# A hybrid encoder trunk with gathered experts: the coefficients of a quarter placed ahead of the routing piece, and a tiny gelu ahead of the first quarter

## The chip, the cores and the metric

The kernel runs on one core of one Trainium2 chip, in fp32. The metric is the device time of one execution in microseconds (us), the median of three runs. In the profile PE is TensorE, ACT is ScalarE, DVE is VectorE, POOL is GpSimd and SP is SyncE; PEld is the weight load of TensorE.

## What is computed

272 tokens (16 learned ones and 256 of the input) of width 1024 pass two layers. Each layer is a mixer and then a PEER expert layer, each with an RMS norm ahead and a residual add behind; one last RMS norm follows. Layer 0's mixer is stick-breaking attention beside a short gated convolution, layer 1's is a Conformer module: a matmul to 2048, a gate, a causal depthwise convolution of 31 taps, a layer norm, silu, and a matmul back. The expert layer, cut to what matters:

```python
q = (y @ w_q).reshape(T, 8, 2, 128)
s = einsum('thpc,pnc->thpn', q, sub_keys)             # two lists of 128 scores a head
val, idx = top_k(s, 16)
cand = val[:, :, 0, :, None] + val[:, :, 1, None, :]  # 16 x 16 pairs
top_val, top_pos = top_k(cand, 16)
expert = take_along_axis(cand_idx, top_pos)           # 16 experts of 16384, a head and token
gate = softmax(top_val)
act = gate * gelu(einsum('thkd,td->thk', u[expert], y))
out = einsum('thk,thkd->td', act, v[expert])
```

## The kernel before, in words

The expert layers are done in steps of 16 tokens: 17 steps for layer 0 (n = 0 to 16) and 16 for layer 1 (n = 17 to 32). In a step the 128 partitions are 8 heads x 16 tokens, and each partition needs 16 experts. GpSimd gathers them one k at a time: one indirect DMA brings for each partition a row of 2048 values, u and v of one expert side by side, 1 MB in all, into one of R = 12 slots of `ring`. A step has four quarters of four k.

**VectorE** runs, for each quarter q of step n, four dots (`dot`, L1197: row u times the token's y, which TensorE has laid out in PSUM, summed into `dots`), each followed by a piece of the mixer's work (`front` for layer 0's attention of later tokens, `side` for the Conformer of the next block of tokens: in its convolution stage two or three taps of L1252). Behind the four dots stands a piece of the routing of later steps: `route_pairs(n + 1)` in quarter 0 (L1157 to L1169), `route_experts(n + 1)` in quarter 1 (L1174 to L1191, which releases the gathers of step n + 1), `finish(n - 2)` in quarter 2 of layer 1 (L1230 to L1235), `route_best(n + 2)` in quarter 3 (L1141 to L1149). Then comes `weights(n, q)`: it waits for the gelu of the quarter, forms `coef` (L1208) and spreads it into `mix` (L1213). In quarter 0 `add_back(n - 1)` follows (L1219), which waits for TensorE's `back`.

**ScalarE** runs `rows(n + 1)` (L456) and `evacuate(n - 1)` (L628: the expert sum out of PSUM into `osb`) at the head of a step, then for each quarter the gelu of four dots (L642), and behind it the mixer's ScalarE work. In the convolution stage that is 20 diagonal matrices a quarter (L569), one for each tap that TensorE does. At the end of a step stand `final_root` (L622, layer 1) and `gates(n + 1)` (L460, an exp). The compiler puts a load of the activation table where the function changes from one table to another.

**TensorE** runs, in a step, `rows(n)` (L833), `values(n - 1, 3)`, `back(n - 1)` (L858), and in each quarter first the mixer's matmuls (`front`, `side`: L668 with streamed weights, L675 column sums, L886 the taps) and then `values(n, q)` (L845), eight matmuls with `mix` against the v halves of four slots. These free the four slots:

```python
mm = pe.matmul(po[32 * j:32 * j + 32, half, :], mix[:, k, :],
               ring[:, slot, D + 512 * half:D + 512 * (half + 1)], start=(q == 0), stop=(q == 3))
if half == 1:
    mm.then_inc(s_vm, 1)
```

**GpSimd** waits for `s_vm` ahead of a gather, and at the first gather of a step also for the expert numbers:

```python
pool.wait_ge(s_idx, n + 1)
for k in range(TOPK):
    i = n * TOPK + k
    if i >= R:
        pool.wait_ge(s_vm, i - R + 1)
```

With 12 slots the gathers 12 to 15 of step n follow `values(n, 0)`, and those 0 to 3 of step n + 1 follow `values(n, 1)`. SyncE streams the mixers' weights in blocks of 512 KB through four buffers. All engines work through their own instructions in the order in which they are written. Layer 1's mixer is computed in two blocks of tokens, in steps 9 to 15 and 17 to 23: the first matmul takes quarters 3 to 6 of such a window, the convolution quarters 7 to 14 (steps 10 quarter 3 to 12 quarter 2, and 18 quarter 3 to 20 quarter 2), mean, variance and silu quarters 15 and 16, the second matmul 17 and 18.

Of the kernel before, what the change touches and what calls it, by code (L numbers as in the profile page):

```python
# [5 lines left out]
P = 128  # L6
# [27 lines left out]
def hybrid_trunk(nc, xT, smalls, wall, uv, out):  # L34
    f32, u32 = mybir.dt.float32, mybir.dt.uint32
    ALU, ACT = mybir.AluOpType, mybir.ActivationFunctionType
# [84 lines left out]
    with ctx:  # L121
        def sb(name, shape, dt=f32):
            return ctx.enter_context(nc.sbuf_tensor(name, shape, dt))
# [37 lines left out]
        epsc = sb("epsc", [P, 1])  # L161
# [18 lines left out]
        grec = sb("grec", [P, 1])  # L180
        dots = sb("dots", [P, TOPK])
        gel = sb("gel", [P, TOPK])
        coef = sb("coef", [P, TOPK])
        mix = sb("mix", [P, TOPK, 2 * GT])
        osb = sb("osb", [P, D])
# [214 lines left out]
        def _(act):  # L400
# [50 lines left out]
            def rows(n):  # L451

                act.wait_ge(s_y, y_ready(n))
                if n:
                    act.wait_ge(s_yr, n)
                act.copy(yg[:, :, :, :], yT[:, :, tokens(n)].unsqueeze(2).to_broadcast([P, C, H, GT])).then_inc(s_yg, 1)  # L456
# [155 lines left out]
            def final(n):  # L612

                act.wait_ge(s_ha, n + 1)
                act.activation(fsq[:, :, :], hT[:, :, tokens(n)], ACT.Square).then_inc(s_fsq, 1)

            def final_root(n):
                m = n - G0
                act.wait_ge(s_fs, m + 1)
                if m:  # L620
                    act.wait_ge(s_fin, m)
                act.activation(frs[:, :], pf, ACT.Sqrt, bias=epsc[:, :], scale=1.0 / D).then_inc(s_frt, 1)  # L622

            def evacuate(n):
                act.wait_ge(s_vm, TOPK * (n + 1))
                if n:
                    act.wait_ge(s_ot, n)
                act.copy(osb[:, :], po.rearrange("p a b -> p (a b)")).then_inc(s_oe, 1)  # L628

            def put(n):  # L630
                m = n - G0
                act.wait_ge(s_fin, m + 1)
                act.dma_start(out[m], fo[:, m % 2, :, :].rearrange("p c t -> p (c t)")).then_inc(s_out[m % 2], 16)

            for n in range(N):
                if n + 1 < N:
                    rows(n + 1)
                if n:
                    evacuate(n - 1)
                for q in range(4):  # L640
                    act.wait_ge(s_dot, TOPK * n + 4 * q + 4)
                    act.activation(gel[:, 4 * q:4 * q + 4], dots[:, 4 * q:4 * q + 4], ACT.Gelu).then_inc(s_gel, 1)  # L642
                    front(4 * n + q)
                    side(n, q)
                    if q == 1 and n > G0:
                        final(n - 1)
                if n > G0:
                    final_root(n - 1)
                if n > G0 + 1:
                    put(n - 2)  # L650
                if n + 1 < N:
                    gates(n + 1)
# [286 lines left out]
        def _(dve):  # L939
# [260 lines left out]
            def weights(n, q):  # L1200

                ks = slice(4 * q, 4 * q + 4)
                if q == 0:
                    dve.wait_ge(s_exp, n + 1)
                    nc.vector.reciprocal(grec[:, :], gsum[:, n % 2:n % 2 + 1])
                    dve.drain()
                dve.wait_ge(s_gel, 4 * n + q + 1)
                nc.vector.scalar_tensor_tensor(out=coef[:, ks], in0=gel[:, ks], scalar=grec[:, :],  # L1208
                                               in1=gexp[:, n % 2, ks], op0=ALU.mult, op1=ALU.mult)
                if n:  # L1210
                    dve.wait_ge(s_vm, TOPK * (n - 1) + 4 * q + 4)
                dve.drain()
                nc.vector.tensor_tensor(mix[:, ks, 0:GT], coef[:, ks].unsqueeze(2).to_broadcast([P, 4, GT]),  # L1213
                                        sel[:, :].unsqueeze(1).to_broadcast([P, 4, GT]), ALU.mult).then_inc(s_m, 1)
# [112 lines left out]
            for n in range(N):  # L1327
                dve.wait_ge(s_yr, n + 1)
                for q in range(4):
                    for i in range(4):  # L1330
                        dot(n, 4 * q + i)
                        front(4 * n + q - 1, i)
                        if q:
                            side(n, q - 1, i)
                        elif n:
                            side(n - 1, 3, i)

                    if q == 0 and n + 1 < N:
                        route_pairs(n + 1)
                    if q == 1 and n + 1 < N:  # L1340
                        route_experts(n + 1)
                    if q == 2 and n > G0 + 1:
                        finish(n - 2)
                    if q == 3 and n + 2 < N:
                        route_best(n + 2)
                    weights(n, q)
                    if q == 0 and n:
                        add_back(n - 1)
                    if q == 2 and n > G0:
                        final_sum(n - 1)  # L1350
# [46 lines left out]
```

## Time and profile before

| what | value |
|---|---|
| median of 3 runs | 1624.63 us (1623.06 to 1624.73) |
| the profiled execution | 1626.37 us, its span 1624.6 us |
| mean granted TensorE clock | 0.774 |
| busy, share of the span | PE 64%, PEld 44%, DVE 69%, ACT 28%, POOL 31% |
| moved by DMA | 649.84 MB, mean 400 GB/s |
| chain that ended last | DMA 40%, PE 26%, DVE 16%, POOL 5%, ACT 5%, issue 5% |

The span is the time from the first to the last instruction of the profiled execution. The shares are means over stages that differ: the first 116 us have no gathers, the steps of layer 0's attention, of the Conformer blocks and the plain steps follow one another. The last line is the chain followed back from the last instruction to what released each piece of work.

### The profile page before, as it was taken

The page shows a single profiled execution, that of the slowest core. Times are in us where ns is not written, and L with a number is a line of the kernel's source. Part 1 is how long each engine was busy: PE and PEld are TensorE (multiplying, and loading weights), DVE is VectorE, ACT ScalarE, POOL GpSimd, SP SyncE. Part 2 cuts the span into 40 slices and gives each one's busy share as a digit, 9 for nine tenths or more (in the row PEclk, how much of TensorE's full clock was granted, in tenths as well). Part 3 has the DMA queues.
Part 4 walks back from the last instruction along what each step waited for, and adds up shares of the span by engine and source line. Part 5 has one row for each costly group of instructions (what it writes and reads, how often), then busy time and mean ns, then how long its engine had stood idle before and what let it go on. Part 6 is the DMA issues. An engine that isn't in the chain of part 4 may idle for free.

```text
span 1624.6 us, 19989 instructions
## 1 busy us (share of the span) xinstructions
PE 1046.7 (64%) x6936; PEld 712.2 (44%) x6936; DVE 1113.1 (69%) x3119; ACT 462.3 (28%) x953; POOL 502.6 (31%) x541
## 2 busy tenths in 40 slices
PE   8996876747644476867573477776576444544454
PEld 8995643525411265756451165655364111211111
DVE  3446768675577765987756765897756777777764
ACT  4101544111011235743121134763222111111110
POOL 0012334322233322333313322332323333333330
PEclk9997868868855799888796579887897566666655
DMA  9969999999999999899999999899999999999994
GB/s 371 355 230 380 417 411 408 419 421 417 418 422 421 421 418 417 352 421 407 420 416 421 421 419 417 353 409 394 415 418 405 422 422 422 421 422 422 421 421 194
DMA packets 106164, 649.84 MB, mean 400 GB/s; under 512 B 11728, under 2 KB 15824, under 8 KB 38480
## 3 DMA queue, kind: packets, MB, share of 16 engines
q0 software_dynamic: 76032, 553.68, 82.4%
q1 hardware_dynamic: 26400, 92.81, 14.7%
q10 hardware_dynamic: 3632, 2.08, 0.4%
q8 instruction: 55, 0.90, 0.2%
q14 instruction: 45, 0.37, 0.1%
HBM read 647.48 MB, written 1.05 MB: 399 GB/s over the span
## 4 chain that ended last, share of the span: by engine, by line
DMA 40%; PE 26%; DVE 16%; POOL 5%; ACT 5%; issue 5%; DVEq 2%; POOLq 0%; ACTq 0%
DMA ring<-in_uv_dram,expert 33%; PE ps L668 13%; DMA wring<-in_wall_dram 8%; DVE ring L1197 7%; PE ps L845 7%; POOL ring L391 5%; ACT side L569 2%; PE ps L858 2%; DVE side L1252 2%; PE ps L675 1%; ACT L460 1%; PE ps L833 1%; DVE picked L1189 1%; DVE mix L1213 1%; PE ps L886 1%
## 5 line engine op out<-in xcount | busy, mean ns | idle before, releaser
L1197 DVE CUSTOM_DVE_ANT_0 ring<-ring,ps 128x1024 f32<-128x1024 f32 x528 | 635.2, 1219 | 321.2 <-DMA ring<-in_uv_dram,expert 250.8
L391 POOL DMA_INDIRECT ring<-in_uv_dram,expert x528 | 500.5, 948 | 1086.6 <-PE ps L845 840.0
L845 PE MATMUL ps<-ring,mix 128*32 128x512 f32 x2112 | 365.6, 827 | 311.4 <-DVE mix L1213 311.2
L845 PEld LDWEIGHTS ps<-ring,mix 128*32 128x32 f32 x2112 | 67.4, 134 | 509.7 <-DVE mix L1213 367.8
L668 PE MATMUL ps<-yT,wring 128*128 128x128 f32 (+1 forms) x1472 | 205.6, 301 | 71.8 <-DMA wring<-in_wall_dram 43.7
L642 ACT ACTIVATE gel<-dots 128x4 f32<-128x4 f32 x132 | 27.1, 205 | 739.2 <-DVE dots L1197 738.8
L668 PEld LDWEIGHTS ps<-yT,wring 128*128 128x128 f32 x1472 | 193.6, 207 | 94.6 <-DMA wring<-in_wall_dram 48.1
L858 PE MATMUL ps<-sel,osb 128*128 128x16 f32 x528 | 84.0, 304 | 78.6 <-ACT osb L628 78.6
L858 PEld LDWEIGHTS ps<-sel,osb 128*128 128x128 f32 x528 | 80.6, 241 | 116.7 <-ACT osb L628 116.7
L569 ACT ACTIVATE side<-ident,params 128x128 f32<-128x128 f32 x310 | 96.5, 389 | 16.0 <-PE ps L886 14.8
L833 PE MATMUL ps<-ident,yg 128*128 128x128 f32 x264 | 49.1, 348 | 71.6 <-DVE dots L1197 71.6
L886 PE MATMUL ps<-side 128*128 128x128 f32 x620 | 83.6, 298 | 2.4 <-ACT side L569 1.8
L886 PEld LDWEIGHTS ps<-side 128*128 128x128 f32 x620 | 79.6, 211 | 10.6 <-issue 10.6
L833 PEld LDWEIGHTS ps<-ident,yg 128*128 128x128 f32 x264 | 41.1, 183 | 73.7 <-issue 73.5
L668 PE MATMUL ps<-yT,ring 128*128 128x128 f32 (+1 forms) x576 | 69.3, 282 | 0.0
L668 PEld LDWEIGHTS ps<-yT,ring 128*128 128x128 f32 x576 | 68.6, 193 | 1.2 <-issue 1.1
L668 PE MATMUL ps<-side,wring 128*128 128x128 f32 (+1 forms) x448 | 59.7, 296 | 10.7 <-ACT side L595 8.1
L642 ACT ACT_TABLE_LOAD x51 | 65.4, 1283 | 1.4
L668 PEld LDWEIGHTS ps<-side,wring 128*128 128x128 f32 x448 | 57.3, 206 | 17.9 <-ACT side L595 10.0
L1252 DVE SCALAR_TENSOR_TENSOR side<-side,params 128x128 f32<-128x128 f32 x180 | 54.2, 349 | 0.0
L628 ACT COPY osb<-ps 128x1024 f32<-128x1024 f32 x33 | 33.3, 1008 | 41.9 <-PE ps L845 41.9
L1197 DVE DVE_READ_ACCUMULATOR2_ANT dots<- 128x1 f32 x528 | 44.0, 83 | 0.0
(207 smaller groups left out, 1043.8 us busy)
## 6 DMA issues: line engine op xcount, KB each, us to landing
wring<-in_wall_dram SPq DMA_DIRECT2D x124, 512.0 KB, 12.2
ring<-in_wall_dram SPq DMA_DIRECT2D x52, 512.0 KB, 13.2
ring<-in_uv_dram,expert POOLq DMA_INDIRECT x528, 16.3
out_dram<-fo ACTq DMA_DIRECT2D x16, 64.0 KB, 6.9
hT<-in_xT_dram ACTq DMA_DIRECT2D x1, 576.0 KB, 15.9
hT<-in_xT_dram SPq DMA_DIRECT2D x2, 256.0 KB, 3.3
params<-in_smalls_dram ACTq DMA_DIRECT2D x1, 380.0 KB, 19.2
params<-in_smalls_dram ACTq DMA_DIRECT2D x1, 50.0 KB, 2.8
```

Of the source, the lines that this page charges most:

```text
L391: pool.indirect_dma_start(out=ring[:, i % R, :], out_offset=None, in_=uv, in_offset=bass.IndirectOffsetOnAxis(ap=expert[:, n % 2, k:k + 1] ...
L460: act.activation(gexp[:, n % 2, :], topv[:, :], ACT.Exp, bias=negm[:, :], accum_out=gsum[:, n % 2:n % 2 + 1]).then_inc(s_exp, 1)
L569: act.activation(diag[:, j % NDIAG, :], ident[:, :], ACT.Identity, scale=convT[:, c, k:k + 1]).then_inc(s_dg, 1)
L628: act.copy(osb[:, :], po.rearrange("p a b -> p (a b)")).then_inc(s_oe, 1)
L642: act.activation(gel[:, 4 * q:4 * q + 4], dots[:, 4 * q:4 * q + 4], ACT.Gelu).then_inc(s_gel, 1)
L668: last = pe.matmul(ps[:, m % 2, 0:w], weights_at(i)[:, c, :], rhs(c), start=(c == 0), stop=(c == C - 1))
L833: last = pe.transpose(yrep[:, c * P:(c + 1) * P], yg[:, c, :, :].rearrange("p h t -> p (h t)"), ident[:, :])
L845: mm = pe.matmul(po[32 * j:32 * j + 32, half, :], mix[:, k, :], ring[:, slot, D + 512 * half:D + 512 * (half + 1)], start=(q == 0), stop=( ...
L858: last = pe.matmul(pt[:, c, :], osb[:, c * P:(c + 1) * P], sel4[:, :], start=True, stop=True)
L886: mm = pe.matmul(ps[:, m % 2, 0:P], diag[:, j % NDIAG, :], gz[:, c, o0 + k:o0 + k + P], start=(k == 0), stop=(k == CK - 1))
L1197: nc.vector.tensor_tensor_reduce(out=row, in0=row, in1=yrep, scale=1.0, scalar=0.0, op0=ALU.mult, op1=ALU.add, accum_out=dots[:, k:k + 1]) ...
L1252: ins = nc.vector.scalar_tensor_tensor(out=cv[:, c, :], in0=src, scalar=tap, in1=cv[:, c, :], op0=ALU.mult, op1=ALU.add)
```

## The change

`weights(n, q)` moves ahead of the routing piece of its quarter, and a gelu of one column (of a constant, into a tile nobody reads) stands on ScalarE at the head of each step, ahead of the first quarter's wait for its dots. Nothing else differs; there are 33 more instructions, all on ScalarE, and as many table loads as before.

```diff
+        warm = sb("warm", [P, 1])
...
                 if n:
                     evacuate(n - 1)
+
+                act.activation(warm[:, :], epsc[:, :], ACT.Gelu)
                 for q in range(4):
                     act.wait_ge(s_dot, TOPK * n + 4 * q + 4)
...
                         elif n:
                             side(n - 1, 3, i)
 
+                    weights(n, q)
                     if q == 0 and n + 1 < N:
                         route_pairs(n + 1)
                     if q == 1 and n + 1 < N:
...
                         finish(n - 2)
                     if q == 3 and n + 2 < N:
                         route_best(n + 2)
-                    weights(n, q)
                     if q == 0 and n:
                         add_back(n - 1)
```

VectorE at the end of step 10 (the third quarter's last taps, `route_best(12)`, the coefficients of quarter 3, the first dot of step 11), before:

```order
L1252 SCALAR_TENSOR_TENSOR side<-side,params 128x128 [waits s_chain] x2
L1141 MAX val<-ps 128x8 [waits s_sc]
L1141 MAX val<-ps 128x8
L1144 MAX_INDEX idx<-val,ps 128x8
L1145 MATCH_REPLACE rest<-val,ps 128x128
L1144 MAX_INDEX idx<-val,ps 128x8
L1145 MATCH_REPLACE rest<-val,ps 128x128
L1149 MAX val<-rest 128x8 x2
L1208 SCALAR_TENSOR_TENSOR coef<-gel,grec,gexp 128x4 [waits s_gel]
L1213 TENSOR_TENSOR mix<-coef,sel 128x4x16 [waits s_vm]
L1197 ISA ring,dots<-ring,ps 128x1024 [waits s_g8,s_yr]
```

The same place on VectorE with the change (lines below the added ones are counted three further):

```order
L1255 SCALAR_TENSOR_TENSOR side<-side,params 128x128 [waits s_chain] x2
L1211 SCALAR_TENSOR_TENSOR coef<-gel,grec,gexp 128x4 [waits s_gel]
L1216 TENSOR_TENSOR mix<-coef,sel 128x4x16 [waits s_vm]
L1144 MAX val<-ps 128x8 [waits s_sc]
L1144 MAX val<-ps 128x8
L1147 MAX_INDEX idx<-val,ps 128x8
L1148 MATCH_REPLACE rest<-val,ps 128x128
L1147 MAX_INDEX idx<-val,ps 128x8
L1148 MATCH_REPLACE rest<-val,ps 128x128
L1152 MAX val<-rest 128x8 x2
L1200 ISA ring,dots<-ring,ps 128x1024 [waits s_g8,s_yr]
```

The pair of `coef` and `mix` has moved up past the whole of `route_best`; the wait for the gelu (s_gel) now stands ahead of the route's rows. In quarter 0 it moves in the same way past the eleven rows of `route_pairs`, in quarter 1 past those of `route_experts`.

ScalarE at the head of step 11, before:

```order
L460 ACTIVATE gexp,gsum<-topv,negm 128x16 [waits s_top]
L456 COPY yg<-yT 128x1024 [waits s_yr,s_y]
L628 COPY osb<-ps 128x1024 [waits s_ot,s_vm]
L642 ACT_TABLE_LOAD
L642 ACTIVATE gel<-dots 128x4 [waits s_dot]
L569 ACTIVATE side<-ident,params 128x128 [waits s_dgu] x20
```

And with the change:

```order
L461 ACTIVATE gexp,gsum<-topv,negm 128x16 [waits s_top]
L457 COPY yg<-yT 128x1024 [waits s_yr,s_y]
L629 COPY osb<-ps 128x1024 [waits s_ot,s_vm]
L642 ACT_TABLE_LOAD
L642 ACTIVATE warm<-epsc 128x1
L645 ACTIVATE gel<-dots 128x4 [waits s_dot]
L570 ACTIVATE side<-ident,params 128x128 [waits s_dgu] x20
```

The table load stands at the same place in both; the tiny gelu comes between it and the gelu of the quarter.

## Rows read from the trace of the kernel before

**Rows 1.** Windows: stretch, its length, busy us by engine, PEclk, DMA share, GB/s

```profile
148.00:151.00 3.00, 0.27 (x4) 0.00 (x0) 2.91 (x7) 0.00 (x0) 1.90 (x3) 0.50 0.45 147
...
1034.00:1039.00 5.00, 5.00 (x45) 3.45 (x44) 4.54 (x14) 4.14 (x15) 0.99 (x1) 1.00 0.13 49
...
1121.00:1123.00 2.00, 0.00 (x0) 0.00 (x0) 2.00 (x4) 1.47 (x4) 1.70 (x2) 1.00 0.36 152
...
1260.00:1600.00 340.00, 161.23 (x780) 59.81 (x772) 245.26 (x655) 59.41 (x105) 124.03 (x132) 0.62 1.01 421
636.00:735.00 99.00, 73.24 (x515) 57.54 (x513) 87.97 (x264) 62.45 (x171) 34.58 (x36) 0.85 0.95 392
...
1014.00:1140.00 126.00, 91.28 (x643) 72.47 (x644) 108.47 (x315) 73.52 (x190) 40.99 (x43) 0.82 0.95 385
```

**Rows 2.** Waits over the whole span: us in total, times, longest us

```profile
POOL ring L391 <- PE ps L845: 840.0, 127, 16.8
...
DVE ring L1197 <- DMA ring<-in_uv_dram,expert: 250.8, 186, 3.6
...
DVE coef L1208 <- ACT gel L642: 14.2, 20, 3.2
```

**Rows 3.** Timeline of ACT, plain step 26: start us, us, instruction, idle before

```profile
1332.72 1.28 ACT L642 ACT_TABLE_LOAD   x1
...
1336.34 0.21 ACT L642 ACTIVATE gel<-dots 128x4 f32<-128x4 f32 x1 [2.33 <-DVE dots L1197]
```

**Rows 4.** Timeline of ACT and DVE, first quarter of work, step 0

```profile
142.86 0.20 ACT L642 ACTIVATE gel<-dots 128x4 f32<-128x4 f32 x1
...
144.26 0.23 DVE L1213 TENSOR_TENSOR mix<-coef,sel 128x64 f32<-128x64 f32 x1
```

**Rows 5.** Timeline of ACT and DVE, end of step 10, first convolution block

```profile
629.26 5.96 ACT L569 ACTIVATE side<-ident,params 128x128 f32<-128x128 f32 x20
...
631.27 0.50 DVE L1141 MAX8 val<-ps 128x8 f32<-128x128 f32 x2 [1.21 <-PE ps L824]
...
633.09 0.49 DVE L1149 MAX8 val<-rest 128x8 f32<-128x128 f32 x2
...
636.53 0.20 ACT L642 ACTIVATE gel<-dots 128x4 f32<-128x4 f32 x1
...
636.77 0.22 DVE L1208 SCALAR_TENSOR_TENSOR coef<-gel,grec,gexp 128x4 f32<-128x4 f32 x1 [3.19 <-ACT gel L642]
...
637.21 1.22 DVE L1197 CUSTOM_DVE_ANT_0 ring<-ring,ps 128x1024 f32<-128x1024 f32 x1
```

**Rows 6.** Timeline of ACT and DVE, quarter 0 of step 11

```profile
644.39 0.09 DVE L1157 MATCH_VALUE_LOAD idx<-val,rest 128x8 f32 x1
...
647.07 0.43 DVE L1169 MAX8 topv<-cand 128x8 f32<-128x256 f32 x1
...
647.44 0.21 ACT L642 ACTIVATE gel<-dots 128x4 f32<-128x4 f32 x1
...
649.82 0.29 DVE L1219 TENSOR_TENSOR hT<-hT,ps 128x128 f32<-128x128 f32 x1 [1.61 <-PE ps L858]
650.02 1.22 DVE L1197 CUSTOM_DVE_ANT_0 ring<-ring,ps 128x1024 f32<-128x1024 f32 x1
```

**Rows 7.** Timeline of DVE and ACT, quarter 1 of step 21, second block

```profile
1125.09 0.42 DVE L1174 FIND_INDEX8 topp<-topv,cand 128x8 uint32<-128x256 f32 x1
...
1126.03 0.21 ACT L642 ACTIVATE gel<-dots 128x4 f32<-128x4 f32 x1
```

**Rows 8.** Timeline of POOL: first gather of four after a wait, at four places

```profile
148.49 0.94 POOL L391 DMA_INDIRECT ring<-in_uv_dram,expert  x1 [8.70 <-PE ps L845]
...
755.56 0.94 POOL L391 DMA_INDIRECT ring<-in_uv_dram,expert  x1 [11.39 <-PE ps L845]
...
1120.95 1.35 POOL L391 DMA_INDIRECT ring<-in_uv_dram,expert  x1 [11.05 <-PE ps L845]
...
1137.42 0.94 POOL L391 DMA_INDIRECT ring<-in_uv_dram,expert  x1 [11.39 <-PE ps L845]
```

## The prediction

> **What bounds the kernel now.** I looked first at the windows, for the share that the DMA engines are busy stage by stage [rows 1]. In the plain steps at the end, 1260 to 1600 us, it is 1.01 at 421 GB/s, while DVE works 245 of 340 us. There a step lasts as long as its 16 MB of gathers take, and VectorE's order cannot matter as long as the next gathers are issued before the queue is empty. In the two convolution stages (636 to 735 and 1014 to 1140 us) the share is 0.95, and DVE is busy 88 of 99 and 108.5 of 126 us. The shortfall lies in short holes: the DMA is at 0.45 in 148 to 151 us, at 0.13 in 1034 to 1039 us, at 0.36 in 1121 to 1123 us. Only in such a hole can a gather that is issued earlier end the kernel earlier, and one that is issued later costs time at once.
>
> Then I read the waits [rows 2]. GpSimd waits 840 us for the matmuls on `ring` that free slots; VectorE waits 250.8 us for gathers, and only 14.2 us for gelus. The last number is the one to look at, since it is small because the routing piece stands between the dots and the coefficients.
>
> **The change, part by part.** *The tiny gelu.* What is the load of its table worth on the path? In a plain step the load starts at 1332.72 us and takes 1.28 us, and the gelu of the quarter starts at 1336.34 us, after 2.33 us in which ACT waited for the dots [rows 3]. The load is already done before the dots are; in the order of before it stands ahead of the wait as well. The Trainium skill says otherwise (page "ScalarE: Activation LUTs", section "Step-by-step: what each stage is for"): the compiler places a table load right before the activation that needs it, and a switch costs about 2.7 us with its drain. By that rule the load would follow the wait, and bringing it early would pay in every step; the trace does not agree with it. By the row, the gain is nothing. The cost is 33 gelus of at most 0.20 us, the length of the gelu of four columns [rows 5]. ACT waits for the dots in the plain steps, which hides it; where ACT is behind, at the heads of some six steps, half of a gelu's length is a fair price, since operations on ACT overlap, and half of these again is covered. **+0.3 us.**
>
> *Coefficients earlier, plain steps.* `mix` comes 0.5 to 4 us earlier, slots come free as much earlier, and the DMA is full anyway. The routing piece ends 0.4 to 0.7 us later, being pushed by the gelu's latency and the two operations: from the start of a gelu to VectorE's next operation behind `mix` it is 636.53 to 637.21, 0.68 us [rows 5]. VectorE has 95 of 340 us free there. **0.**
>
> *The first step.* The gelu starts at 142.86 us and `mix` at 144.26 us [rows 4]. With 0.68 less 0.14 us behind the gelu `mix` would start at 143.4 us, 0.8 us earlier. The gathers that this frees start at 148.49 us, after 8.70 us of waiting [rows 8], and the DMA is nearly idle then. **-0.8 us.** VectorE itself comes out later, since `route_pairs` now stands behind the gelu that ACT delays; but its own next gathers have three in the queue ahead of them.
>
> *The convolution stages.* ACT is the late engine here: it builds 20 diagonals a quarter, 5.96 us each time [rows 5], and a gelu stands behind them. VectorE used these waits for routing. At the end of step 10 `route_best` ran from 631.27 to 633.58 us and VectorE then waited 3.19 us more for the gelu of 636.53 us [rows 5]. With the change it waits all the time and runs `route_best`'s 2.3 us afterwards, so the dots of step 11 begin 2.2 us later than 637.21 us. That alone is hidden, because the next gelu is set by ACT at 647.44 us, 3 us after `route_pairs` began, so later still behind the dots [rows 6]. But the same happens again there: `route_pairs` ran from 644.39 to about 647.5 us, before that gelu. Now it follows: 647.44 + 0.1 (tiny gelu) + 0.68 + 3.1 + 0.2 (from the add of L1219 to the dot) = 651.5 us instead of 650.02 us, **+1.5 us**. `back` was ready at 649.82 us, so it doesn't hide this [rows 6]; the wait of 1.61 us for it goes away, and `route_pairs` takes its place.
>
> Who waits? The dots of the next quarters, and behind them the gelu, and behind the gelu in ACT's order the next 20 diagonals, `gates` and `evacuate`, and behind these TensorE's `back`, taps and `values`. Earlier coefficients don't help here, since `values` stands behind the taps on TensorE. In step 12 (or 20) the shift is about 1.7 us, and the head of step 13 (or 20 already, where `route_pairs` was hidden altogether) adds 1.4 us more: 3.1 to 3.2 us. In quarter 1 of step 21 the gelu of 1126.03 us is again ACT's, and `route_experts`, which began at 1125.09 us [rows 7], moves behind it: 1126.03 + 0.68 - 1125.09, less the 0.6 that `coef` and `mix` took anyway, is **+1.0 us** more. The second matmul's results wait for VectorE behind that.
>
> What it costs is read where gathers are short. In the second block the first gather after a wait is at 1120.95 us, when the DMA is already in its hole [rows 1, 8]; 3.2 us later is 3.2 us lost, and the next, at 1137.42 us, is 4.2 us later, some of which the weight blocks fill. I take **+3.4 us**, with bounds of 1.5 (if half is absorbed, as in the first block) and 4.5. In the first block the like place is at 755.56 us [rows 8], 2.9 us later; the DMA is full until then, so I take half of it, **+1.5 us**, with bounds of 0 and 3. The hole of 1034 to 1039 us stays as it is: its gelus are ACT's and their `values` stand behind the taps.
>
> Sum: +0.3 - 0.8 + 3.4 + 1.5 = **+4.4 us**. On the profiled execution of 1626.37 us that gives 1630.8 us; the median of the runs is 1.7 us lower, so it is **1629.0 us**. The order at the very end (the last quarter has no routing piece) is the same, and the tail with it.
>
> **The rivals.** *Hidden: no change.* The DMA holds the time from end to end, and VectorE's shifts are taken up by the row of slots that are filled ahead. For it: VectorE is idle in every stage, and the DMA is 40% of the chain that ended last. Against it: the holes, where the queue is empty and the shift passes through. It decides if more than two thirds of the shift of 3 to 4 us is absorbed in each block. Time: from -0.8 + 0.3 to 1.5 us more, 1624 to 1626 us.
>
> *Faster: the holes close.* Slots come free up to 4 us earlier. If the holes were `mix`'s, the change would fill them: 0.55 of 3 us at 148, 0.64 of 2 us at 1121, 0.87 of 5 us at 1034 and as much again in the first block, 1.7 + 1.3 + 2 x 4.4 = 11.7 us at most [rows 1]. Most of these follow `values` that stood behind taps, not behind `mix`; I would give it 4 to 5 us, 1620 us. It decides if TensorE turns out to reach `values` before `mix` is there.
>
> *Faster: the table.* If the load of 1.28 us [rows 3] did sit behind the dots, the eight steps in which VectorE, ACT and TensorE set the pace (0, 1, 11 to 13, 19 to 21) would gain it each: 10 us, 1614 us. The rows speak against it. The rule of the Trainium skill named above would lead here.
>
> *Much slower.* No absorption anywhere: both blocks at 4.2 us and the delay of attention's first steps, some 2.3 us, as well: 1635 us.
>
> **How the numbers follow.** About 0.2% (3.2 us) is what a measurement of this kernel can tell from no change. Forecast (+3.3 to +8 us) 0.56, hidden 0.30, holes close 0.09 (of it 0.02 within 0.2%), table 0.01, much slower 0.04. So slower 0.60, same 0.32, faster 0.08. The range takes in the forecast with its bounds (-0.8 + 0.3 + 1.5 + 0 = +1.0 to +7.0, and 1 more for what I may have missed in the attention steps) and the hidden case: 1623.5 to 1633.0 us.
>
> **What would show it.** VectorE's wait for gelus must grow from 14.2 us to 40 or more. The wait of `add_back` for `back` must go in steps 11, 13, 19 to 21. The gathers of 1120.95 and 1137.42 us must come about 3 and 4 us later against those of 1034 to 1039 us, the hole in front of them must widen, and the plain steps must keep 1.01 and 421 GB/s. Table loads: as many, as early as now. I am wrong if the two blocks last as long as before, or if the first gather behind 1100 us comes earlier.

## The result, and the profile after

| what | before | after |
|---|---|---|
| median (runs) | 1624.27 us (6 runs, 1623.06 to 1625.49) | 1635.07 us (6 runs, 1630.73 to 1636.16) |
| ratio to before, 95% interval | | 1.0064 (1.0051 to 1.0077) |
| the profiled execution, its span | 1626.37, 1624.6 us | 1634.59, 1632.9 us |
| granted TensorE clock | 0.774 | 0.781 |
| VectorE's wait for gelus | 14.2 us, 20 times | 63.1 us, 104 times |
| table loads for the gelus | 51 | 51 |

The change makes the kernel slower by 0.64%: 10.8 us by the medians, 8.3 us by the spans of the two profiled executions. The forecast was +4.4 us and its range ended at 1633.0 us: the sign and the place were right, the size was not.

Windows of the kernel after, the stretches of [rows 1] (stretch, its length, busy us by engine, PEclk, DMA share, GB/s):

```profile
148.00:151.00 3.00, 0.00 (x0) 0.00 (x0) 2.86 (x9) 0.00 (x0) 2.39 (x3) 0.50 0.55 147
636.00:735.00 99.00, 72.24 (x509) 56.79 (x508) 87.06 (x267) 63.25 (x174) 34.82 (x36) 0.84 0.96 393
...
1126.00:1128.00 2.00, 1.46 (x16) 0.24 (x8) 1.97 (x3) 1.10 (x2) 0.28 (x1) 1.00 0.03 12
1128.00:1130.00 2.00, 0.00 (x0) 0.00 (x0) 2.00 (x3) 2.00 (x6) 1.69 (x2) 1.00 0.38 53
...
1014.00:1140.00 126.00, 84.36 (x599) 66.69 (x599) 104.09 (x312) 75.52 (x197) 39.44 (x41) 0.84 0.93 376
...
1260.00:1600.00 340.00, 153.26 (x784) 57.09 (x787) 247.81 (x670) 62.45 (x116) 126.44 (x135) 0.64 1.01 421
```

The plain steps keep 1.01 and 421 GB/s, as forecast. The stretch of the first convolution is the same within 0.01, that of the second fell from 0.95 to 0.93 of the DMA's time: 2% of 126 us is 2.5 us, and more lies behind 1140 us. The hole in front of the gather (21,3) is wider: it was 0.36 in 1121 to 1123 us, and is now 0.03 in 1126 to 1128 and 0.38 in 1128 to 1130 us.

Waits after (engine line, what it waited for, us in total, times, longest), which answer to [rows 2]:

```profile
ACT gel L645 <- DVE dots L1200: 799.3, 114, 12.5
POOL ring L392 <- PE ps L848: 743.0, 110, 16.0
...
DVE ring L1200 <- DMA ring<-in_uv_dram,expert: 242.2, 190, 3.8
POOL ring L392 <- DVE expert L1194: 220.8, 19, 113.2
...
DVE coef L1211 <- ACT gel L645: 63.1, 104, 6.7
```

The wait for gelus has grown by 49 us, in 84 more places. GpSimd's wait for `values` fell by 97 us, and it now waits 19 times for the expert numbers instead of once (113.0 and now 113.2 us of it before the first gather): slots do come free earlier, and at the head of 18 steps the first gather then stands for `route_experts`, which the change has put behind the coefficients.

### The profile page after: what moved, and what is told of

It reads as the page before. It is cut to its first block, busy times and chain, and to the rows that moved or that the text cites. A ratio compares the mean times of both kernels' runs of the same rounds, so it can differ in the third digit from the quotient of the medians.

```text
span 1632.9 us, 20023 instructions
## 1 busy us (share of the span) xinstructions
PE 1052.5 (64%) x6936; PEld 719.9 (44%) x6936; DVE 1115.4 (68%) x3119; ACT 466.2 (29%) x986; POOL 500.1 (31%) x541
## 4 chain that ended last, share of the span: by engine, by line
DMA 42%; PE 25%; DVE 15%; ACT 7%; POOL 5%; issue 4%; DVEq 1%; POOLq 0%; ACTq 0%
DMA ring<-in_uv_dram,expert 37%; PE ps L671 13%; DVE ring L1200 8%; DMA wring<-in_wall_dram 6%; POOL ring L392 5%; PE ps L848 5%; ACT side L570 2%; PE ps L861 2%; DVE side L1255 1%; PE ps L678 1%; PE ps L836 1%; PE ps L889 1%; ACT osb L629 1%; ACT L461 1%; DVE picked L1192 1%
## 5 line engine op out<-in xcount | busy, mean ns | idle before, releaser
L671 PE MATMUL ps<-yT,wring 128*128 128x128 f32 (+1 forms) x1472 | 213.6, 309 | 67.5 <-DMA wring<-in_wall_dram 35.7
L671 PEld LDWEIGHTS ps<-yT,wring 128*128 128x128 f32 x1472 | 201.9, 215 | 88.8 <-DMA wring<-in_wall_dram 42.3
L1211 DVE SCALAR_TENSOR_TENSOR coef<-gel,grec,gexp 128x4 f32<-128x4 f32 x132 | 29.3, 222 | 65.1 <-ACT gel L645 63.1
L678 PE MATMUL ps<-side,ones 128*128 128x128 f32 (+1 forms) x144 | 29.3, 385 | 25.3 <-ACT side L600 13.8
```

Of the source, the lines that this page charges most:

```text
L671: last = pe.matmul(ps[:, m % 2, 0:w], weights_at(i)[:, c, :], rhs(c), start=(c == 0), stop=(c == C - 1))
L678: last = pe.matmul(ps[:, m % 2, 0:w], ones[:, :], src[:, c, 0:w], start=(c == 0), stop=(c == C - 1))
```

## Where the time came from

The first gather of a group of four is a good clock of progress, since it can't be issued before slots are free. Its time in the two traces, from the timelines of GpSimd (step and quarter of the gathered experts):

| gather | before | after | later by |
|---|---|---|---|
| 11, 3 | 659.32 | 659.29 | 0.0 |
| 14, 0 | 755.56 | 758.43 | 2.9 |
| 16, 0 | 854.56 | 855.28 | 0.7 |
| 20, 1 | 1051.31 | 1053.39 | 2.1 |
| 20, 3 | 1078.76 | 1082.68 | 3.9 |
| 21, 3 | 1120.95 | 1127.72 | 6.8 |
| 22, 0 | 1137.42 | 1146.73 | 9.3 |
| 32, 3 (the last four) | 1585.33 | 1593.59 | 8.3 |

Up to the end of the first block most is as forecast, and only the gain of the first step doesn't last: the 0.6 us won in the first step (148.49 to 147.90 us) is gone at 659 us, the gather of 755.56 us comes 2.9 us later, and the full DMA behind it takes most of that back. The second block does not: 7.2 us are lost between the gathers (20,1) and (22,0) alone, where 3.4 us were forecast for the whole block.

The head of step 20, quarter 0, before (the order's own wait for `back`, in front of the first dot of quarter 1):

```profile
1067.54 0.21 ACT L642 ACTIVATE gel<-dots 128x4 f32<-128x4 f32 x1
...
1067.67 0.43 DVE L1169 MAX8 topv<-cand 128x8 f32<-128x256 f32 x1
...
1069.91 0.29 DVE L1219 TENSOR_TENSOR hT<-hT,ps 128x128 f32<-128x128 f32 x1 [1.15 <-PE ps L858]
1070.12 1.21 DVE L1197 CUSTOM_DVE_ANT_0 ring<-ring,ps 128x1024 f32<-128x1024 f32 x1
```

The same place after:

```profile
1070.34 1.28 ACT L642 ACT_TABLE_LOAD   x1
1071.63 0.20 ACT L642 ACTIVATE warm<-epsc 128x1 f32<-128x1 f32 x1
1071.74 0.19 ACT L645 ACTIVATE gel<-dots 128x4 f32<-128x4 f32 x1
...
1071.96 0.22 DVE L1211 SCALAR_TENSOR_TENSOR coef<-gel,grec,gexp 128x4 f32<-128x4 f32 x1 [3.04 <-ACT gel L645]
...
1075.27 0.43 DVE L1172 MAX8 topv<-cand 128x8 f32<-128x256 f32 x1
1075.61 0.27 DVE L1222 TENSOR_TENSOR hT<-hT,ps 128x128 f32<-128x128 f32 x1
1075.80 1.22 DVE L1200 CUSTOM_DVE_ANT_0 ring<-ring,ps 128x1024 f32<-128x1024 f32 x1
```

From the gelu to the next dot it was 2.58 us and is 4.06 us. Before, all of `route_pairs` but its last MAX8 had run when the gelu started; now the 3.04 us of waiting that held it are empty, and its 3.1 us follow. That is the forecast mechanism, and at step 11 it has the forecast size (the dot of [rows 6] moves from 650.02 to 651.57 us). But the gelu itself is 4.20 us later here, which the forecast did not have. The same reading at the places where ScalarE brings the gelu late:

| place | gelu later by | next dot later by |
|---|---|---|
| step 10, q1 | 0.2 | 1.6 |
| step 11, q0 | 0.1 | 1.6 |
| step 12, q0 | 1.8 | 1.8 |
| step 13, q0 | 1.4 | 2.9 |
| step 13, q1 | 1.6 | 2.9 |
| step 18, q1 | 1.3 | 2.8 |
| step 19, q0 | 2.6 | 4.1 |
| step 20, q0 | 4.2 | 5.7 |
| step 21, q0 | 6.6 | 8.0 |
| step 21, q1 | 6.4 | 7.7 |

Of these places four in the first block and five in the second add 1.2 to 1.5 us to the shift that they find; step 12 adds none. In the first block that of step 10 is gone by the next gelu (615.46 us in both traces). In the second, 1.3 us were there on entry, and the shifts of step 18 to the head of step 21 stay and come one on top of the other. In quarter 3 of steps 10 and 18 VectorE comes 2.2 us later as well, but the next gelu does not. In quarter 1 of steps 11, 19 and 20 VectorE was as late already, and at most 0.3 us are added. The second block's heads are longer on ScalarE, since `final_root` (a table load of 1.28 us and 0.28 us) stands there too, and `route_pairs` lay almost wholly within the wait at each of them. And step 19 is entered with 2.6 us: in quarter 1 of step 18, in the stage of the first matmul, `route_experts` filled such a wait as well (the gelu of 977.27 us came 2.5 us behind its dots), and the forecast has no term for it. The next matmul of the mixer on TensorE starts 2.4 us later there (984.69 and 987.09 us); by which wait the shift reached it was not followed.

Then quarter 1 of step 21, where the second matmul's chunks go through two PSUM banks. Timeline of TensorE before:

```profile
1124.77 5.47 PE L668 MATMUL ps<-side,wring 128*128 128x128 f32 x32 [4.07 <-ACT side L595]
1131.01 3.81 PE L668 MATMUL ps<-side,wring 128*128 128x128 f32 x32 [0.77 <-DVEq L1309]
1134.74 1.92 PE L845 MATMUL ps<-ring,mix 128*32 128x512 f32 x16
```

and after:

```profile
1131.21 3.84 PE L671 MATMUL ps<-side,wring 128*128 128x128 f32 x32 [3.76 <-ACT side L596]
1138.69 5.44 PE L671 MATMUL ps<-side,wring 128*128 128x128 f32 x32 [3.63 <-DVEq L1312]
1144.05 1.92 PE L848 MATMUL ps<-ring,mix 128*32 128x512 f32 x16
```

A group of 32 is two chunks. The second two wait until VectorE has read the banks of the first two, which it does between the dots of quarter 2, behind `route_experts`. From start to start of the two groups it was 6.24 us and is 7.48 us, 1.24 us more, and that is what VectorE comes later behind the gelu (gelu to next dot 3.29 us before, 4.53 us after). The wait in brackets has grown by more, 0.77 to 3.63 us, since the first group was quicker; and the second now takes 5.44 instead of 3.81 us. The gathers of step 22 wait for the `values` behind it. Timeline of GpSimd after (the like of the last line of [rows 8]):

```profile
1127.72 1.03 POOL L392 DMA_INDIRECT ring<-in_uv_dram,expert  x1 [11.37 <-PE ps L848]
...
1146.73 0.94 POOL L392 DMA_INDIRECT ring<-in_uv_dram,expert  x1 [14.26 <-PE ps L848]
```

## The experiments

Most are the changed kernel with the place of `weights(n, q)` chosen quarter by quarter, the tiny gelu kept:

```diff
-                    weights(n, q)
+                    early = CONDITION
+                    if early:
+                        weights(n, q)
                     if q == 0 and n + 1 < N:
                         route_pairs(n + 1)
...
                         route_best(n + 2)
+                    if not early:
+                        weights(n, q)
```

The chips differ: in the first four runs and the last two the kernel before took 1625.2 and 1624.75 us, in the others 1632.4 to 1633.2 us. Every ratio is to the kernel before on the same chip. Beside the ratio I read two stretches from each trace: **A**, from the gather (20,1) to (21,3), which holds the head of step 20 and that of step 21 up to its first coefficients, and **B**, from (21,3) to (22,0), which holds quarter 1 of step 21. Most of the 8 us between the chips lie ahead of both, but A is not free of it: with the old order there it is 70.5 us on the faster chips (mean of 5 traces) and 71.8 us on the slower (4).

### Which part, and where

```diff
-                act.activation(warm[:, :], epsc[:, :], ACT.Gelu)
```

with `early = True`:

> The change without the tiny gelu: only the coefficients placed ahead of the routing piece. Theory A (VectorE now waits, in the two convolution blocks, for gelus that ScalarE has late, and does its routing afterwards): the whole loss stays, 8 to 11 us over before, 1633 to 1635 us, the first gather behind 1120 us of before again 6 to 7 us late. Theory B (ScalarE's extra operation at the head of a step carries the loss, since ScalarE is the late engine in the blocks): most of it goes, 1624 to 1627 us.

`early = False`, the tiny gelu kept:

> The tiny gelu alone, the order of before. Theory A: 33 operations of 0.2 us, mostly where ScalarE waits anyway, and the table load as early as before: 1624 to 1625 us, no change. Theory B: slower by 5 us or more.

`early = n not in (10, 11, 12, 13, 18, 19, 20, 21)`:

> The change's order everywhere except in steps 10 to 13 and 18 to 21, which have the order of before; with the tiny gelu. Theory A: the loss is made in these eight steps only, so 1623 to 1626 us. Rival C (the delay of VectorE adds up over all steps, the attention steps above all): 3 us or more slower than before, 1628 us or more.

`early = n in (10, 11, 12, 13, 18, 19, 20, 21)`:

> The reverse: the change's order in steps 10 to 13 and 18 to 21 only. Theory A: the whole loss, 1632 to 1635 us. Rival C: less than half of it, under 1629 us.

| kernel | median, us | ratio (95%) | A, us | B, us |
|---|---|---|---|---|
| before | 1625.2 | | 69.64 | 16.47 |
| after | 1635.07 | 1.0064 (1.0051 to 1.0077) | 74.33 | 19.01 |
| e1, order only | 1631.15 | 1.0048 (1.0031 to 1.0064) | 72.48 | 17.71 |
| e2, tiny gelu only | 1624.98 | 1.0002 (0.9994 to 1.0011) | 69.20 | 16.46 |
| e3, outside the blocks | 1624.1 | 0.9994 (0.9985 to 1.0003) | 71.12 | 16.29 |
| e4, inside the blocks | 1634.45 | 1.0060 (1.0046 to 1.0073) | 74.14 | 19.09 |

The order inside eight steps makes the loss by itself. In the other 25 steps it makes no difference that can be measured, and neither does the tiny gelu alone. Whether the gelu adds something to the order stays open: e1 is 0.16% under the change, the intervals overlap, and in e1's trace the second group of B's matmuls ran at the higher clock, which is part of the distance (below).

### Which block, which quarter

`early = n in (18, 19, 20, 21)`:

> The change's order in steps 18 to 21 only (second convolution block), tiny gelu as in the change. The prediction gave the second block 3.4 us and the first 1.5. From the trace of the change, where the gathers are 1.5 us late behind the first block and 8 to 9 behind the second: about 6 to 7 us over before here, 1631 us. If the two blocks only add up in the way that the prediction had them: 1628.5 us.

`early = n in (10, 11, 12, 13)`:

> The change's order in steps 10 to 13 only (first block). 1.5 to 2.5 us over before, 1626 to 1627.5 us. If the blocks weigh the same: 4 to 5 us.

The steps of both blocks, quarter 0 alone:

> The change's order in steps 10 to 13 and 18 to 21, in quarter 0 alone: the coefficients ahead of route_pairs. The prediction puts the shifts there: three times 1.5 us in a block (steps 11, 12, 13), one of them absorbed by the layer norm's wait, so 3 us at the hole and over half of the loss: 1628 to 1631 us. If the late release of the second matmul's banks behind route_experts in quarter 1 of steps 13 and 21 is the larger part: under 1627 us.

and quarter 1 alone:

> The same in quarter 1 alone: the coefficients ahead of route_experts. By the prediction 1 us in a block: 1625.5 to 1627 us. If TensorE's wait for VectorE in quarter 1 of step 21 (3.63 us with the change, 0.77 before) is the quarter's own doing: 1628 us or more.

| kernel | median, us | ratio (95%) | A, us | B, us |
|---|---|---|---|---|
| e5, second block | 1638.91 | 1.0034 (1.0020 to 1.0049) | 72.54 | 17.71 |
| e6, first block | 1633.38 | 1.0004 (0.9992 to 1.0015) | 71.45 | 16.22 |
| e7, quarters 0 | 1634.58 | 1.0014 (1.0003 to 1.0025) | 73.56 | 16.05 |
| e8, quarters 1 | 1636.21 | 1.0025 (1.0015 to 1.0036) | 71.65 | 19.34 |

The second block costs 0.34%, 5.5 us; the first 0.04%, which is 0.6 us and can't be told from nothing. Both are under what had been expected of them, and e7's 0.14% (2.3 us) is under the half of the loss that was expected of quarter 0. Quarter 1 costs at least as much as quarter 0, and the stretches separate them cleanly: e7 lengthens A and leaves B, e8 lengthens B by 2.9 us and has A where the old order has it (e6). A and B are one trace each.

### Quarter 1 of step 21

`early = (n, q) not in ((13, 1), (21, 1))`:

> The whole change, but in quarter 1 of steps 13 and 21 (the second matmul of each Conformer block) the coefficients stay behind route_experts, as before. Theory P (route_experts behind the late gelu makes TensorE's second pair of chunks wait 3.63 us for VectorE's bank release instead of 0.77, and run at the low clock, 5.44 instead of 3.81 us): the wait returns to about 1 us, the second pair to 3.8 us, values(21,1) come 3 to 5 us earlier than with the change against values(21,0), and the time is about 1629 to 1631 us on a chip where the change takes 1635. Rival S (the delay is a plain sum of shifts of about 1 us spread over all quarters of the blocks): these two quarters give back at most 1.5 us, 1633.5 us or more.

`early = (n, q) == (21, 1)`:

> The order of before everywhere but in quarter 1 of step 21, which has the order of the change. Theory P: this one place costs 1 us of VectorE's shift, 1 to 3 us of TensorE's wait and 1.6 us if the pair falls to the low clock: 1626.5 to 1629 us where before takes 1624.6. Rival S: at most 1 us, 1625.6 us. Rival C (the loss at this place needs the shift collected in steps 18 to 20): no change, 1624.6 us, and the second pair stays at 3.8 us.

The change, and `route_experts` moved away from in front of the bank release:

```diff
-                    if q == 1 and n + 1 < N:
+                    if q == 1 and n + 1 < N and n not in (13, 21):
                         route_experts(n + 1)
...
                         elif n:
                             side(n - 1, 3, i)
+                        if n in (13, 21) and q == 2 and i == 1:
+                            route_experts(n + 1)
```

> The change, but route_experts for steps 14 and 22 is moved from behind the dots of quarter 1 to behind the second dot of quarter 2 and its piece of the mixer, so that both PSUM banks are released ahead of it. Theory P (the bank release behind route_experts is the cause in quarter 1 of step 21): TensorE's second pair of chunks waits under 1 us instead of 3.63, gathers (21,3) to (22,0) are 16.5 us or less instead of 19.0, and the time is 2 to 3 us under f0. Rival E (route_experts itself then comes too late for the gathers of step 22): GpSimd's first gather of step 22 waits for expert instead of values, and the time is that of f0 or more. Rival S (spread): no change against f0.

The change itself once more, beside it on the same chip:

> The change itself, so that the next three stand beside it on one chip. If this is the chip of the first runs: ratio 1.006 to the kernel before. On the slower chip, where parts of the change cost 0.04% to 0.34%: 1.003 to 1.004, and the stretch from gather (21,3) to gather (22,0) is 19 us as in the change's first profile (16.5 before).

| kernel | median, us | ratio (95%) | A, us | B, us |
|---|---|---|---|---|
| e9, the change without the two quarters | 1635.79 | 1.0025 (1.0011 to 1.0039) | 72.56 | 16.46 |
| e10, one quarter alone | 1636.5 | 1.0019 (1.0005 to 1.0032) | 71.89 | 18.91 |
| f0, the change again | 1640.46 | 1.0045 (1.0029 to 1.0060) | 72.72 | 17.71 |
| f1, the change, experts later | 1637.26 | 1.0023 (1.0006 to 1.0040) | 74.05 | 15.30 |

In e9 the wait of TensorE's second group is 0.76 us and the group takes 3.81 us, as theory P had it. Its ratio is 0.20% under that of f0, on another chip, and the intervals overlap. One quarter of one step, moved by itself (e10), costs 0.19% (3.1 us); theory P gave 1.9 to 4.4 us for it. B of f0 is 17.71 us and not the 19 that had been expected, since its second group ran at the higher clock. Timeline of TensorE in e10:

```profile
1132.92 3.84 PE L671 MATMUL ps<-side,wring 128*128 128x128 f32 x32 [3.65 <-ACT side L596]
1140.40 5.44 PE L671 MATMUL ps<-side,wring 128*128 128x128 f32 x32 [3.64 <-DVEq L1312]
```

and in f1:

```profile
1134.52 9.04 PE L671 MATMUL ps<-side,wring 128*128 128x128 f32 x64 [3.91 <-ACT side L596]
1143.49 1.92 PE L848 MATMUL ps<-ring,mix 128*32 128x512 f32 x16
```

e10 shows the change's lines with nothing else moved, so the shift collected in steps 18 to 20 is not needed for it. In f1 the wait is gone: the four chunks run as one group of 64 in 9.04 us, where before they took 10.05 us from the start of the first group to the end of the second, and after 12.92 us. B falls to 15.30 us, under that of the kernel before, and rival E (the expert numbers come too late) doesn't hold: GpSimd waits there 10.39 us for `values`. f1 is 3.2 us under f0 by the medians, as theory P had it; the intervals of the two ratios overlap a little, the stretches don't.

### The other places

`early` everywhere but in ten quarters, 1 of step 10, 0 of 11 to 13, 1 of 13, 1 of 18, 0 of 19 to 21, 1 of 21:

> The change with the order of before in ten quarters: 1 of step 10, 0 of steps 11 to 13, 1 of step 13, and the same in the second block (18, 19 to 21, 21), where the routing piece stood in the wait for a gelu that ScalarE holds up. Theory K (these places carry the whole loss, each q0 +1.5 us on VectorE, quarter 1 +1.5 and +2.5): the time of before within 1.5 us. Rival S (every quarter of the blocks adds a little, the ones with route_best and the plain ones too): at least a third of f0's loss stays, 2 us or more on either chip.

`early` in those ten alone:

> The order of before with the order of the change in those ten quarters alone. Theory K: the time of f0 within 1.5 us, VectorE's first dot of quarter 1 of step 21 (behind add_back) 6 us or more later against gather (18,0) than before. Rival S: at most two thirds of f0's loss.

f2 took 1634.51 us, ratio 1.0007 (0.9993 to 1.0020), A 72.35, B 16.47 us. f3 took 1636.55 us, ratio 1.0026 (1.0012 to 1.0041), A 73.54, B 17.23 us. With the ten places put back, 1.1 us of loss is left and can't be told from nothing, as theory K had it: 122 of the 132 quarters can have the order of the change without a loss that is measured (the interval ends at 3.3 us). But the ten alone give 4.2 of f0's 7.3 us, which is what rival S allowed (at most two thirds) and less than K asked for. So neither account is whole. The ten places are needed for the loss; whether the neighbours, harmless by themselves, make the same ten cost more, or the 3 us between f3 and f0 are chance (their intervals overlap), stays open.

### Two attempts at a better kernel

TensorE reaches `values(n, q)` behind 20 taps in the convolution, so an early `mix` is of no use there. With `values` ahead of the taps, on top of the change:

```diff
+                    first = q < 3 and 7 <= window(n, q)[1] < 15
+                    if first:
+                        values(n, q)
                     side(n, q)
-                    if q < 3:
+                    if q < 3 and not first:
                         values(n, q)
```

> The change, and on TensorE values(n, q) stand ahead of the taps of their quarter while the convolution runs (quarters 0 to 2 of steps 11, 12, 19, 20). Here the earlier mix can be used: if the holes of the DMA at 655 to 661 and 1034 to 1039 us (0.13 of its share) come from values standing behind 20 taps, they close and give back some 4 us each, and the loss of the change in these steps with them: 1622 to 1630 us where the change takes 1635. If what bounds these stages is ScalarE's and TensorE's taps, the taps come 1.9 us a quarter later and the time is 1635 us or more.

and on top of the kernel before:

> The kernel before, with TensorE's values ahead of the taps in the same quarters. If the holes are closed by the order on TensorE: 1616 to 1622 us, and no loss from the routing pieces, which stay ahead of the coefficients. If VectorE's mix behind route_pairs is what holds the values there (the reason for the change under its own theory), the gain is 1 to 3 us less than e11 has against the change. If the taps bound: 1625 us or more.

1657.31 us, ratio 1.0155 (1.0132 to 1.0178), and 1656.67 us, ratio 1.0142 (1.0123 to 1.0161): 23 to 25 us slower, with either order of VectorE. Timeline of TensorE and ScalarE in e12, quarter 2 of step 19:

```profile
1069.52 3.64 PE L847 MATMUL ps<-ring,mix 128*32 128x512 f32 x16 [4.59 <-DVE mix L1218]
...
1073.92 0.73 ACT L570 ACTIVATE side<-ident,params 128x128 f32<-128x128 f32 x2 [5.02 <-PE ps L888]
```

TensorE now stands 4.59 us for `mix`, does `values` at the low clock (3.64 instead of 1.92 us), and ScalarE waits 5.02 us behind it because its diagonals have no free buffer until the taps use them. From the gather (20,0) to (20,1) it is 12.38 us, against 6.55 before. So in the kernel before the taps in front of `values` filled the wait for `mix`. That the hole of 1034 to 1039 us is the price of this order is likely, but no run shows it apart.

From f1's stretch B came two more. The kernel before, without the tiny gelu, with `route_experts` for steps 14 and 22 moved as in f1:

> The kernel before with one thing moved: route_experts for steps 14 and 22 stands behind the second dot of quarter 2 and its piece of the mixer. From the profile of f1, where gather (21,3) to (22,0) took 15.3 us against 16.5 us before: 1.2 us less in the second block and at most as much in the first, which in the first block may be absorbed: 1 to 2.4 us less than before, ratio 0.9985 to 0.9994. Rival E (route_experts becomes the late one for the gathers of step 22): the gather (22,0) waits for expert, no gain or a loss of up to 1 us.

and the same with the change's order and the tiny gelu outside the eight steps:

> The same, with the change's order and tiny gelu outside steps 10 to 13 and 18 to 21, where it made a ratio of 0.9994 [0.9985, 1.0003]. If that was a real gain: 0.5 to 1 us under g1. If it was noise: the time of g1 within 0.1%.

1625.12 us, ratio 1.0003 (0.9994 to 1.0012), and 1625.23 us, ratio 1.0000 (0.9991 to 1.0009). B is 15.22 and 15.18 us, the 1.2 us less that f1 promised, and the time is that of before. The stretch A ends later in them than in the one trace of before (71.4 against 69.64 us), and in the traces with the old order A lies anywhere from 69.2 to 71.9 us, so a gain of 1.2 us at one place is smaller than that spread. The 1 to 2.4 us that had been expected did not come: the two intervals end at 1.0 and 1.5 us under before. No version beats the kernel before.

## Why the prediction was wrong in size

**The step that failed is the second block's term**, +3.4 us with bounds of 1.5 and 4.5. Alone it measures 5.5 us (e5), an interval of 3.3 to 8.0 us that only just takes in the forecast. The traces of the chips at 1625 us say more. From the gather (18,1), which lies ahead of the block's first late gelu, to (22,0) the old order took 195.0, 195.2 and 195.3 us (before, e2, e3), the change's order 200.3 us with the second matmul's second group at the high clock (e1) and 202.6 and 202.8 us with it at the low (the change, e4). That is 5.2 us more, or 7.5 us. Two parts of the term were undersized, for different reasons.

On the slower chips the same stretch took 196.8 us (e6, old order) and 199.7 and 199.2 us (e5, f0): 2.4 to 2.9 us more, within the forecast's bounds, though f0 costs 7.3 us by its runs. Where the rest of f0's loss lies, and why the chips differ, stays open. The parts that were measured singly (e2, e6 and e5: 0.3, 0.6 and 5.5 us) add up to 6.4 us.

*Quarter 1 of step 21*, put at +1.0 us on VectorE. As a shift that was nearly right: in all eight traces with the new order there (e11 and e12, whose TensorE order differs, left out here and below) TensorE's second group starts 7.47 or 7.48 us after the first, in the seven with the old 6.22 to 6.27 us, so 1.24 us later. What the forecast lacked is what TensorE does with it: in four of the eight the second group then ran partly at the low clock, 1.63 us more. B is 16.35 us with the old order (mean of 7), 17.6 us with the new at the high clock (4), 19.1 us at the low (4), and 15.2 us where `route_experts` stands behind the release (3). The change's trace is one of the long ones, 2.5 us, and e10 costs 3.1 us.

*The heads.* I took the shift of 1.5 us once, 0.2 more in step 20 and 1.4 at the next head, 3.1 us in all, on the reasoning that the gelus are ScalarE's and do not move. They move: at steps 20 and 21 ScalarE's chain starts behind the last gelu of the step before, and that one waits for dots (2.24 and 8.05 us in the change's trace). So each head of the second block added its 1.5 us to the shift it found, to 4.1, 5.7 and 8.0 us; 1.3 us of these were there on entry, and quarter 1 of step 18, which the forecast left out, gave 1.4 us. In gathers, from (18,1) to (21,3), the old order took 178.5 to 180.0 us (before, e2, e3, g1, g2) and the new 182.6 to 183.7 us (the change, e1, e4): 4.3 us by the means, where the forecast had 3.2 us. The mean of A alone goes from 70.5 to 73.7 us on these chips and from 71.8 to 73.2 us on the slower (4 and 6 traces, of kernels that differ elsewhere), so the larger size is shown for the faster chips alone.

**What was right.** *The first block*, +1.5 us with bounds of 0 and 3, was right within its bounds: e6 has +0.6 us, with an interval from -1.3 to +2.4 us, and the gather of 755.56 us moved by 2.9 us, the number forecast. *The plain steps*, 0: e3. *The tiny gelu*, +0.3 us: e2 has +0.3 us, with -1.0 to +1.8. The table load is where it was: in the plain step whose gelu now starts at 1344.65 us the load is at 1340.14 us, and the gelu comes after 3.02 us of waiting for dots.

```profile
1340.14 1.28 ACT L642 ACT_TABLE_LOAD   x1
1341.43 0.20 ACT L642 ACTIVATE warm<-epsc 128x1 f32<-128x1 f32 x1
1344.65 0.20 ACT L645 ACTIVATE gel<-dots 128x4 f32<-128x4 f32 x1 [3.02 <-DVE dots L1200]
```

The load runs ahead of the wait in both versions, takes 1.28 us with the next operation right behind it, and e2 gains nothing. The Trainium skill (page "ScalarE: Activation LUTs", section "Step-by-step: what each stage is for") has a load right before the activation that needs it and about 2.7 us for it with its drain. The order of the instructions agrees with the first; the second the trace doesn't bear out. The page does not say on which side of a semaphore wait the load falls: that the prediction's rival put it behind the wait was a reading of the page, which the trace refutes.

*The first step*, -0.8 us, was right as an issue time (-0.6 us) and wrong as a gain. By the gather (11,3) nothing of it was left, and e3, which has it, is not measurably faster. What paces the steps of attention behind it I did not follow.

The rival **much slower**, 1635 us, is nearest to the result, by luck, since the reason is another than it had: not the absence of absorption in the first block and a delay in attention's first steps, but a second block in which shifts add up. Its chance of 0.04 rested on ScalarE's gelus as fixed points. The signs named in advance came: VectorE's wait for gelus is over 40 us, the wait of `add_back` is gone in steps 11, 13 and 19 to 21, the hole in front of them widened, and the two gathers came later, against that of 1037.74 us (now 1039.39 us) by 5.1 and 7.7 us instead of 3 and 4.

## What to carry to other kernels

A long piece of work that fills an engine's wait for a late partner is not in the way, even if something short and urgent stands behind it. Moving the short thing ahead empties the wait, and the piece then costs its length at each such place, less what it still hides: of `route_pairs`' 3.1 us 1.5 us came through here, since it took the place of a wait for `back` of 1.2 to 1.6 us. Before such a move, list every place where the short thing's input is late, follow the shift round the whole loop (VectorE, ScalarE, VectorE) until it meets an engine that really has slack, and do not take the partner's times as fixed.

Ask also of each moved piece which releases stand behind it: here a bank release behind the routing made TensorE's next group start 1.24 us later, and 1.6 us of clock could come on top. And where an engine that works in order has other work ahead of a waiting instruction, putting the waiting one first can cost more than the hole it is to close: 23 us here.

## What the runs showed of the hardware

**The granted clock after a wait.** The same 32 matmuls of the second matmul took 3.81 to 3.84 or 5.44 to 5.47 us. Windows of before and after, each within one such group:

```profile
1125.00:1130.00 5.00, 5.00 (x32) 5.00 (x31) 4.47 (x14) 1.42 (x3) 0.94 (x1) 0.66 0.99 342
1131.00:1134.50 3.50, 3.49 (x31) 3.50 (x32) 2.99 (x6) 0.00 (x0) 0.00 (x0) 1.00 1.01 422
```

```profile
1131.50:1134.50 3.00, 3.00 (x29) 3.00 (x29) 1.40 (x8) 1.37 (x3) 0.94 (x1) 1.00 0.99 396
1139.00:1144.00 5.00, 5.00 (x32) 4.93 (x30) 3.98 (x8) 0.20 (x1) 0.00 (x0) 0.66 1.00 370
```

Before, the first group is at a mean of 0.66 (part of it at 1.2 GHz) and the second at 1.00 (2.4 GHz); after, it is the other way round. In the eight traces with the new order at this place the second group took 5.43 or 5.44 us in four (after, e4, e8, e10; B 18.9 to 19.3 us) and 3.81 us in four (e1, e5, f0, f3; B 17.2 to 17.7 us). I found nothing in what TensorE did just before that tells the two apart: e4 and e5 both have a first group of 5.47 us and a wait of 2.01 us. So 1.6 us of the change's loss depends on how the clock falls, and the runs of e1, 1629.7 to 1631.7 us four times and 1635.5 us twice, look like such a split. That the clock makes it is not shown, as only one run of each kernel has a trace.

**A small gain can be lost in the spread of a stretch.** With VectorE's order the same, stretch A took from 69.2 to 71.4 us in five traces on the faster chips, and 71.5 and 71.9 us in two on the slower. What makes this spread no run shows. A local gain of 1.2 us (B of g1 and g2) in a block whose DMA share is 0.95 can be read plainly in the timeline and still not be found in the time.
